# A transformer layer on one Trainium2 core: the next segment's preparation placed among the present segment's inverse levels, the inverse on one bank pair, no reciprocal in the matrix memory's norm

## The reference

```python
for l in range(DEPTH):
    x = x + 0.5 * _swiglu(_rmsnorm(x, ffn1_norm[l]), ...)
    x = x + _token_mix(_rmsnorm(x, mix_norm[l]), w_in[l], ...)
    x = x + _memory_attention(_rmsnorm(x, xa_norm[l]), _rmsnorm(mem, mem_norm[l]), ...)
    x = x + 0.5 * _swiglu(_rmsnorm(x, ffn2_norm[l]), ...)
return _rmsnorm(x, final_norm)
# in _token_mix, RWKV-7:
decay = exp(-exp(-softplus(-w_raw) - 0.5));  a = sigmoid(a0 + a_d @ a2);  g = sigmoid(g_d) @ g2
kk = kf * k_k / max(norm(kf * k_k), 1e-12);  k_mod = kf * (1 + (a - 1) * k_a)
S_t = S_{t-1} diag(w_t) + (S_{t-1} (-kk_t)) (kk_t a_t)^T + v_t k_t^T;   y_t = S_t r_t
# mLSTM, stabilised and chunkwise:
h = num / max(|den|, exp(-m_row));   h = (h - mean(h)) * rsqrt(var(h) + 1e-6)
```

## Time and profile before

| | |
|---|---|
| median of three runs | 2966.72 us |
| span of the profiled execution, its only time shown | 2967.3 us |
| PE busy | 2849.2 us, 96% |
| DVE, POOL, ACT busy | 1354.6, 1246.7, 564.3 us |
| the mixers, first `lora` to the last `Wst` | 1102.97 to 1681.14 us |
| an ordinary segment, `Wst` to `Wst` | 69.85 us |

### The profile page before, as it was taken

One profiled execution on the slowest core, in us unless ns is written; L12 is line 12 of the kernel. 1 busy time (PEld: TensorE's weight loads), 2 busy tenths in 40 slices (PEclk: granted clock), 3 DMA queues, 4 the chain that ended last, 5 costly groups with the idle time before them and its releaser, 6 DMA issues.

```text
span 2967.3 us, 36791 instructions
## 1 busy us (share of the span) xinstructions
PE 2849.2 (96%) x14694; PEld 2359.7 (80%) x14694; DVE 1354.6 (46%) x1109; ACT 564.3 (19%) x793; POOL 1246.7 (42%) x627
## 2 busy tenths in 40 slices
PE   7999999999999998999999999998899999999996
PEld 5888888888788877777777778888788888888885
DVE  5431331234556535776777555543344322331334
ACT  3100010012000112443444232214321100100011
POOL 3433344433694623555555443321043344433331
PEclk9999999999999999998999999999999999999998
DMA  3111111112762554444434164122011111111111
GB/s 133 43 50 50 50 49 45 48 46 103 298 247 92 192 194 149 101 107 139 102 102 104 61 223 149 51 75 102 8 43 50 49 50 47 46 49 50 50 41 73
DMA packets 115401, 271.35 MB, mean 91 GB/s; under 512 B 7644, under 2 KB 58972, under 8 KB 108272
## 3 DMA queue, kind: packets, MB, share of 16 engines
q1 hardware_dynamic: 93504, 210.79, 22.4%
q10 hardware_dynamic: 21808, 59.27, 5.3%
HBM read 207.56 MB, written 62.44 MB: 91 GB/s over the span
## 4 chain that ended last, share of the span: by engine, by line
PE 79%; issue 9%; POOL 6%; DVE 4%; ACT 1%; DMA 0%; SPq 0%; POOLq 0%; DVEq 0%; ACTq 0%
PE G L755 24%; PE G L757 24%; PE G L756 24%; PE G L879 2%; POOL AL L686 2%; PE G L1164 1%; PE G L916 1%; POOL Tr L680 1%; ACT sx L1559 0%; DVE nt_a L1644 0%; DVE mx L2008 0%; DVE px L2016 0%; POOL rho L669 0%; PE G L1156 0%; PE G L820 0%
## 5 line engine op out<-in xcount | busy, mean ns | idle before, releaser
L719 POOL TENSOR_TENSOR whi<-raw,zero 128x1024 fp32r<-128x1024 f32 (+1 forms) x199 | 378.2, 1900 | 1312.8 <-PE G L757 1233.2
L755 PE MATMUL G<-hhi,whi 128*128 128x512 f32 x2032 | 794.0, 391 | 21.0 <-DVE hlo L1650 17.9
L757 PE MATMUL G<-hhi,wlo 128*128 128x512 f32 x2032 | 791.8, 390 | 0.0
L756 PE MATMUL G<-hlo,whi 128*128 128x512 f32 x2032 | 791.5, 390 | 0.0
L722 POOL TENSOR_TENSOR wlo<-raw,whi 128x1024 fp32r<-128x1024 f32 (+1 forms) x199 | 482.6, 2425 | 15.6
L755 PEld LDWEIGHTS G<-hhi,whi 128*128 128x128 f32 x2032 | 382.1, 188 | 104.2 <-issue 13.0
L757 PEld LDWEIGHTS G<-hhi,wlo 128*128 128x128 f32 x2032 | 382.1, 188 | 79.8
L756 PEld LDWEIGHTS G<-hlo,whi 128*128 128x128 f32 x2032 | 382.2, 188 | 79.6 <-issue 0.7
L755 PE MATMUL G<-ahi,whi 128*128 128x512 f32 x960 | 374.8, 390 | 2.7 <-DVEq L457 2.7
L756 PE MATMUL G<-alo,whi 128*128 128x512 f32 x960 | 374.2, 390 | 0.0
L757 PE MATMUL G<-ahi,wlo 128*128 128x512 f32 x960 | 374.1, 390 | 0.0
(11 more groups left out here) (329 smaller groups left out, 3301.8 us busy)
## 6 DMA issues: line engine op xcount, KB each, us to landing
gw<-gw_d SPq DMA_DIRECT2D x32, 1024.0 KB, 5.3
raw<-in_wg SPq DMA_DIRECT2D x44, 512.0 KB, 3.2
raw<-in_wu SPq DMA_DIRECT2D x44, 512.0 KB, 3.3
raw<-in_wd SPq DMA_DIRECT2D x32, 512.0 KB, 3.3
gw_d<-gw SPq DMA_DIRECT2D x16, 1024.0 KB, 4.8
graw<-in_gates_in SPq DMA_DIRECT2D x16, 512.0 KB, 7.2
raw<-in_ml_in SPq DMA_DIRECT2D x16, 512.0 KB, 3.7
zml_d<-po ACTq DMA_DIRECT2D x16, 512.0 KB, 2.6
```

The lines of the kernel that those rows point to most:

```text
L719: nc.gpsimd.tensor_tensor(whi[:, k, 0:w], raw[:, k, 0:w], zero[:].to_broadcast([P, w]), ALU.add).then_inc(hi_made, 1)
L755: nc.tensor.matmul(dst, wh, hi, start=start, stop=False)
L756: nc.tensor.matmul(dst, wh, lo, start=False, stop=False)
L757: return nc.tensor.matmul(dst, wl, hi, start=False, stop=stop)
```

## The change

Three things are changed, all in the mixers.

1. The preparation of segment i + 1 (all steps from `lora` to the first mask `am0`, `am1`, `T0`) no longer stands at the start of its own segment but inside iteration i: `lora` after level 1, `tw` in level 2, `ta` in level 3, the decay sums in levels 3 and 4, `kmod` in level 4, `rinv`, `alpha`, `beta` in level 5, score `A` behind `UQ`. The turns of `alpha`, `beta`, `kap` and the values, and `B`, `Mu`, `Mv`, move in among the levels too. The loads of the RWKV inputs are three instead of one. The back part of segment i - 1 moves: `gate` and the C and N updates to the start of the next iteration, the output's newton steps behind `U6`. The table `slots` is new, with the same 72 (48) fills.
2. `W{n}` and `E{n}` are both written to G1 (before: `W{n}` to G1, `E{n}` to G0); PE's transposes go to G0.
3. The matrix memory's `h` is no longer divided by `max(|den|, exp(-m))`. The mean is taken off `num` itself, and the square of the divisor, times 1e-6, is added to the variance: two `max` on DVE (`dm`, `dd`) and a square on ACT (`sqd`) in place of an absolute value, a maximum, two reciprocals and a constant. `m` is kept at or above -28.

```diff
-            for n in range(1, LEVELS):                                    # PE, before
-                eight(g1, AL[:, n % 2], Ur).then_inc(*F.sig(f"W{n}"))
...
-                if n == 3:
-                    pe.wait_ge(*m_act.at("aden", i))
...
-                eight(g0, Tr, Wr).then_inc(*F.sig(f"E{n}"))
-                gates(f"b{n}")
+            level_e(2)                                                    # PE, after
+            gates("b2")
+            level_w(3)
+            pe.wait_ge(*l_pool.at("kap", i))
+            if more:
+                pe.wait_ge(*l_act.at("ta", i + 1))
+            gram(kap, alpha, g0).then_inc(*F.sig("B"))
+            if more:
+                if back:
+                    pe.wait_ge(*b_dve.at("yc", j))
+                keys_ahead(i + 1)
+            gates("a3")
+            level_e(3)
...
+            gates("b3")
+            level_w(4)
+            if back:
+                variance()
+            pe.wait_ge(*f_dve.at("B", i))
+            pe.wait_ge(*f_pool.at("rho", i))
+            gram(beta, rho, g0).then_inc(*F.sig("Mu"))
+            gates("a4")
+            level_e(4)
+            pe.wait_ge(*m_dve.at("dd", i))
+            for h in range(MH):      # num
...
+            gates("b4")
+            level_w(5)
...
-        slots[0] = {**slots[0], "s1": unit, "s2": unit, "s3": unit, "s4": 6, "s5": 8, "s6": 10}
+        usual = dict(s1=6, s2=2, b1=2, b2=8, a3=6, b3=4, a4=6, b4=3, a5=6, b5=5, a6=8, b6=6, F=10)
+            level(3)                                                      # ACT, after
+            if more:
+                rate_lora(i + 1)
+                log_exp_tables()
+            level(4)
...
+            level(6)
+            token("v", vtok, g2[:, 0, :])
+            turned(6)
+            token("k", ktok, g2[:, 1, :])
+            update(3)                                                     # DVE, after
+            gate_part(0)
...
+                decay_sums(i + 1)
+            dve.wait_ge(*f_pe.at("B", i))
+            gram(Bm, g0, C_UP).then_inc(*F.sig("B"))
+            if more:
+                decay_centred(i + 1)
+            update(4)
...
+            stt(flat(aden[:]), m0, 1.0, flat(nmb[:]), ALU.mult, ALU.max).then_inc(*M.sig("dm"))
+            dve.wait_ge(*M.at("dm", i))
+            stt(flat(aden[:]), m0, -1.0, flat(aden[:]), ALU.mult, ALU.max).then_inc(*M.sig("dd"))
...
-                    nc.vector.reciprocal(aden[:, 0:2], aden[:, 0:2]).then_inc(*M.sig("rec0"))
+        def kap_ahead(i):                                                 # POOL, after
+            pool.wait_ge(*l_act.at("Pi", i))
+            pool.wait_ge(*l_dve.at("kmod", i))
+            pool.wait_ge(*f_act.at("ktok", i - 1))
+            tt(kap[:], kmod[:], Pi[:, :, 1:DEC], ALU.mult).then_inc(*l_pool.sig("kap"))
...
+            if more:
+                kap_ahead(i + 1)
             pool.wait_ge(*f_dve.at(f"U{LEVELS - 1}", i))
             tt(Uf[:], copies(C_ID), Ur[:].bitcast(F32), ALU.subtract).then_inc(*F.sig("IU"))
+            if back:
+                output()
```

More of the change, by code:

```diff
@@ L111 @@
[L111 to L116, removed]
+L_PE = ["lora", "ss", "A"]
@@ new lines @@
+L_ACT = ["th", "ad", "gt", "tw", "ta", "P", "Pi", "lnn", "rinv"]
+L_DVE = ["dec", "scan", "hend", "cc", "ssc", "av", "gu", "kmod", "n1", "n2", "rin", "kk", "kka", "alpha", "beta", "A",
+         "arg", "am0"]
+L_POOL = ["kkr", "sq", "kap", "am1", "T0"]
+F_PE = ["am0T", "W1", "E1", "W2", "E2", "W3", "B", "E3", "W4", "Mu", "E4", "W5", "aT", "bT", "Mv", "E5", "W6", "V5",
+        "vT", "kT", "E6", "F", "V6", "bonus", "UQ", "Wst", "Z"]
+F_ACT = ["Wc1", "Wc2", "Tc1", "Wc3", "Tc2", "Wc4", "Tc3", "Wc5", "Tc4", "atok", "btok", "Wc6", "Tc5", "vtok", "Tc6",
+         "ktok", "W1c", "Zc"]
@@ L117 @@
+F_DVE = ["U0", "U1", "T1", "gs", "U2", "T2", "U3", "T3", "S0s", "pend", "B", "U4", "T4", "Mu", "U5", "Mv", "U6", "Q",
+         "bv", "Uf"]
+F_POOL = ["am2", "am3", "rk", "rkb", "rho", "am4", "am5", "am6", "IU"]
+B_PE = ["U", "gate", "Y", "dS", "mean", "var"]
+B_ACT = ["Un", "gev", "Y0", "Y1", "lnv", "rsv"]
 B_DVE = ["dS", "S", "yc", "ve", "g1", "g2", "g3", "y1"]
-B_POOL = ["bvb", "ysq", "y2", "y3", "y4"]
-M_PE = ["kT", "vT", "S", "den", "num", "mean", "var", "dC", "dN"]
-M_ACT = ["gtok", "ktok", "E", "nm", "vtok", "D", "aden", "lnv", "rsv"]
@@ L989, in iteration @@
[L989 to L1000 removed]
+                if back:
+                    pe.wait_ge(*m_dve.at("C", j))
+                    pe.wait_ge(*b_act.at("gev", j))
@@ new lines, in iteration @@
+            pe.wait_ge(*f_dve.at("B", i))
[4 more added lines that the diff above has]
+            pe.wait_ge(*m_dve.at("dd", i))
+            for h in range(MH):
+                dst = m0[:, h * SEG:(h + 1) * SEG]
+                nc.tensor.matmul(dst, mvtok[:, h, :], Pb[:, h, :], start=True, stop=False)
+                last = nc.tensor.matmul(dst, CN[:, 0, h, :], qe[:, h, :], start=False, stop=True)
@@ new lines, in iteration @@
+            last.then_inc(*M.sig("num"))
+            gates("b4")
+            level_w(5)
+            if more:
+                pe.wait_ge(*l_dve.at("ssc", i + 1))
+            elif back:
+                pe.wait_ge(*b_dve.at("yc", j))
+            turn(g2[:, 0, :], alpha).then_inc(*F.sig("aT"))
+            if back:
+                pe.wait_ge(*b_dve.at("ve", j))
+            turn(g2[:, 1, :], beta).then_inc(*F.sig("bT"))
+            pe.wait_ge(*f_dve.at("Mu", i))
+            gram(kap, rho, g0).then_inc(*F.sig("Mv"))
@@ L1067, in iteration @@
+            nc.tensor.matmul(g2[:, 0, :], con(C_HONES), flat(rkb[:]), start=True, stop=True).then_inc(*F.sig("bonus"))
             gates("F")
-            pe.wait_ge(*f_act.at(f"Tc{LEVELS - 1}", i))
+            pe.wait_ge(*f_act.at("Tc6", i))
             pe.wait_ge(*f_dve.at("Q", i))
@@ L1071, in iteration @@
             if more:
-                ahead(i + 1)
+                gram_ahead(i + 1)
+            pe.wait_ge(*m_dve.at("ve", i))
+            pe.wait_ge(*m_pool.at("kw", i))
+            for h in range(MH):
+                last = nc.tensor.matmul(m0[:, h * SEG:(h + 1) * SEG], kw[:, h, :], con(C_ONES), start=True, stop=True)
+            last.then_inc(*M.sig("dN"))
+            pe.wait_ge(*f_act.at("ktok", i))
             pe.wait_ge(*f_dve.at("Uf", i))
```

809 lines of the change are left out of this document (456 added, 353 removed).

## The result

| | before | after |
|---|---|---|
| median | 2967.01 us (2966.01 to 2969.22, 4 runs) | 3107.69 us (3103.95 to 3108.87, 4 runs) |
| profiled execution, span | 2967.3 us | 3107.1 us |
| mean granted clock of TensorE | 0.986 | 0.961 |

The change makes the kernel slower: the ratio is 1.0473, 95% interval 1.0458 to 1.0488. The forecast of 3031 us (2984 to 3068) had the sign and most of the places, and less than half of the size: 64 us were forecast and 140 were lost.

The account below looks back on a forecast made before the run. PE, busy for 96% of the span, was taken to bound the kernel, so only its work or waits could give time. The profiled 2967.3 us + 42 of net waits + 22 for the clock gave 3031 us, range 2984 to 3068.

Parts of the forecast that it names:

- The clock: Over the mixers, 14 of 22 long PE waits each bring a clock fall costing 1.6 us: +22 us.
- rival 1: All 22 long waits bring a clock fall: 3044 us, up to 3070 if it stays low longer; chance 0.22.
- The steps that I looked at and found covered: In the mixers, am0, U6, the RWKV input loads and broadcast rows come in time behind PE's work: no wait.
- a long wait [...] where I have none: Sign of a wrong prediction: in a middle segment, a long wait at an unforecast place, at a DMA above all.
- its +12: Segment 0: the same new waits plus some 5.5 us uncovered in the first levels, less some 6: +12 us.
- Waits a, c and d: New PE waits in an ordinary segment: B for ta 2.9 us, num for dd 3.6, UQ for Q 3.5.
- Wait b: In an ordinary segment, PE's b3 and Mu wait for DVE: 1.0 us, then 1.2 more; 2.1 in all.
- the forecast's +6.4 for a segment: Ordinary segment: 12.1 us of new waits less 5.7 of old ones; +32 us over five such segments.
- parts 2 and 3 are worth nothing: The one bank pair costs nothing; missing reciprocals free some 4 us of DVE a segment, alone worth nothing or within 5.7.
- 75.4 against 76.57: -1: Segment 3: 64.1 - 5.6 + 12.1 + 4.8 = 75.4 us after the change, against 76.57 before: -1 us.
- 42 forecast: Net added waiting: five ordinary segments +32 us, segment 0 +12, segments 3 and 7 -1 each.
- These 5.7 us a segment are all that a better order of the same work can win: Ordinary segment: about 5.7 us lost to waits, 3.74 of it visible, beside 64.1 us of PE work; the most to win.

Follow-up runs that it names:

- e4_gs: Changed kernel with gs on DVE ahead of U1, not behind T1 and qe: 3072.48 us, ratio 1.0349 to the kernel before.
- e12_g1: Kernel before the change, with only E{n} written to G1 as W{n} is: 2968.54 us, ratio 1.0002.
- e15_norec_act: Kernel before the change, with only the reciprocals dropped, the divisor's square on ACT and the row step at -28: 2965.40 us, ratio 1.0001.
- e17_ssc: e13_dd with the read of ss (ssc) on DVE right behind the centred sums, ahead of U4: 2957.09 us, ratio 0.9968 to the kernel before.
- e7_ss1: Changed kernel with the next segment's product ss moved from behind B to between E4 and num's wait: 3092.81 us, ratio 1.0418 to the kernel before.
- e2_num: Changed kernel with dm and dd on DVE ahead of U4 and T4: 3062.19 us, ratio 1.0317 to the kernel before.
- e3_iu: Changed kernel with the next segment's kap on POOL behind IU, not ahead of it: 3068.54 us, ratio 1.0341 to the kernel before.
- e13_dd: Changed kernel with ta, IU, gs, Bm, am0, ten fills and fill unit reordered, dm and dd right behind Bm: 2959.77 us, ratio 0.9974 to the kernel before.

## Why the prediction was wrong

- *The clock*, "14 x 1.6 = +22", is the step that failed by most: 64.4 us. Both factors were too small. All 22 of the long waits that were forecast brought a fall, as rival 1 ("every long wait costs the clock") had it, and so did the 6 that were missed: 64.4 / 28 = 2.3. The 1.6 was read rightly from the earlier trace rows, but it is the price of a short stretch: the clock there is 0.57 over 4.00 us, so 3.4 us at the low level, as behind `ta`, where the waits of `num`, `UQ` and `S` mostly had 6.8. Rival 1 was the nearest, but its 3044 to 3070 used the same 1.6. The window over that place in the kernel before:

```profile
1104.00:1108.00 4.00, 4.00 (x13) 0.57 0.23 70
```

- *"The steps that I looked at and found covered"* failed too: the list left out `gsr`. I followed what PE's products need, back to their makers, and did not ask what a moved step (`decay_inputs`) waits for and what then stands behind it on ACT. It is a wait for a buffer to come free, 3.44 to 3.46 us in five segments and 2.24 in segment 4, 19.5 in all, and worth 35 us (e4_gs). The prediction had named "a long wait [...] where I have none" as a sign that it was wrong; it stood at an ACT copy, not at a DMA. `am0`, which the list has as covered, made PE wait 2.0 us in segment 4; the 3.7 us in segment 0 are within its +12.
- *Waits a, c and d* were right in place and cause, and nearly in size: visible 2.7 to 2.9, 3.4 and 3.3 forecast, 2.75, 3.36 and 2.89 measured. *Wait b* was right in its first part (1.0, measured 0.93) and not in its second: before `rho,beta` 0.19 was left of "about 1". `dec` took 0.42 us there, not the 0.83 of the earlier trace rows, and `S0s` and `pend` together 0.4, not 0.8. The four together are 10.1 us of visible waiting against 3.7 before, which is the forecast's +6.4 for a segment. That parts 2 and 3 are worth nothing was right too, on the kernel before (e12_g1, e15_norec_act).
- *Segment 3*, "75.4 against 76.57: -1", is a wrong sum. The 76.57 hold some 9 us of low clock (21.00 us at a mean of 0.51, PE busy for 18.15 of them), which the 75.4 leave out. So it set 16.9 us of waits against some 9 of waits, which is +8, and called it -1. Measured without the missed wait: +7.5.
- With the missed wait taken out, the idle time grew by 56 of the 75.6 us, against 42 forecast. The largest part of the difference is segment 3.
- *"These 5.7 us a segment are all that a better order of the same work can win"* holds for ordinary segments (e17_ssc wins 2.9 of them in segment 2). It fails for segment 3, which e17_ssc does in 66.6 us, 10 less than before, most of it by the clock (mean 0.97 against 0.87).
- Segments 4 (94.4 us) and 0 (26 us more) were forecast as ordinary and as +12. Segment 0's idle time grew by the 12 that were forecast; most of the rest is the clock. Segment 4 has no fills in its first levels, and `am0` stands behind rows that lie in the queue behind the 14.5 us load of `hq`; 13.7 us at the low clock follow there.

The clock, the missed wait, segment 3 and `am0` all made the kernel slower than forecast; only the second part of wait b went the other way, by some 1 us a segment. So no large error hid another.

What stays open: when a wait brings a fall and how long it lasts. All 28 long waits of the changed kernel did, but one of 2.45 us in e7_ss1 and some of 2.89 and 3.36 in e2_num, e3_iu and e4_gs did not. That is one reason why no single price fits: a wait cost 1.7 to 1.8 times its length in the changed kernel and 1.35 and 1.56 in e13_dd. The other is that other waits grow or shrink with it. Part 2 and part 3 were tried on the kernel before only.

## What to carry to other kernels

Price a wait of a busy TensorE by its length and the low clock behind it; in this kernel the second came to 64 us beside 76 of the first. When a step is moved up an engine's list, look at every condition that it waits for, buffers that must come free above all, and at what stands behind it there. An idle gap may also be what keeps two engines' instructions off each other, so a wait taken away can come back in another place: run it, and read the lengths of the instructions again.

## What the runs showed of the hardware

- All 28 waits of PE of 2.2 to 5.2 us (for `dd`, `Q`, `mvtok` and `ta`) had a stretch at a granted clock of 0.50 in or behind them, of 3.4 or 6.8 us. Shorter waits sometimes did: those of 1.9 us in e13_dd in six of seven segments. And one of 2.45 us in e7_ss1 did not. Filling the gaps before `num` with useless matmuls made the kernel 8.5 us faster.
- DVE instructions with two SBUF inputs beside one of POOL's masks of 2.4 us: `S0s` 0.41 became 2.18, the scan 1.23 became 3.27, even `pend` (4 columns) 0.15 became 2.34. One with one SBUF and one PSUM input (`Bm`) kept its length, 1.31.
- A single SBUF input does not keep a DVE instruction free of it: the `tensor_scalar` `gsig`, SBUF to SBUF, 0.22 alone, took 1.28 beside POOL's `rkb`, and `hend` (4 columns) 0.17 alone, took 1.53 beside a mask (1347.89 in the changed kernel). The reciprocal of the kernel before, SBUF to SBUF too, began 1.06 us ahead of a mask that kept its 2.38.
- It works the other way as well: a mask took 2.81 behind DVE's square, 2.38 behind its reciprocal.
